# The inverse of the delta rule in 32-column diagonal blocks and corners, in place of 128-column products at every level

## The chip, the cores and the metric

The kernel is one program for one core of one Trainium2 chip. All data are fp32, except a few mask constants in bf16. The metric is the device time of one execution on that core in microseconds; a smaller number is better. Three executions of the kernel before took 4603.44, 4605.32 and 4605.34 us; their median is 4605.32 us.

TensorE (PE) multiplies a stationary block, which a weight load (PEld) brings in, with a moving block, and writes to PSUM. In this trace every fp32 product is two weight loads and two matmuls; a transpose with the identity is one of each. VectorE (DVE), ScalarE (ACT) and GpSimd (POOL) do elementwise work. Engines wait for each other by semaphores only.

## The reference, cut to what matters

The program runs a chain of stages: a modulation stage (Ada), a gated-delta-rule mixer (DeltaNet), Peer, attention, Peer, and then a second model part. The change touches the delta rule alone. Per head and per chunk of tokens the reference does

```python
gc = jnp.cumsum(gc, axis=-1)
decay = jnp.exp(jnp.where(incl, gc[..., :, None] - gc[..., None, :], -jnp.inf))
kk = jnp.einsum('bhid,bhjd->bhij', kc, kc)
a = eye + jnp.where(strict, kk * decay * bc[..., :, None], 0.0)
rhs = jnp.concatenate([vc * bc[..., None], kc * (bc * jnp.exp(gc))[..., None]], axis=-1)
sol = lax.linalg.triangular_solve(a, rhs, left_side=True, lower=True, unit_diagonal=True)
u, w = sol[..., :dv], sol[..., dv:]
v_new = u - jnp.einsum('bhcd,bhde->bhce', w, S)
qk = jnp.where(incl, jnp.einsum('bhid,bhjd->bhij', qc, kc) * decay, 0.0)
o = q_exp_gc @ S + qk @ v_new            # written as einsums
S = S * jnp.exp(g_last)[..., None] + k_decayed.T @ v_new
```

16 value heads of 128 channels, 512 tokens (256 context, 256 latent), forward and backward. The kernel takes chunks of 128 tokens, so there are four chunks per direction.

## The kernel before, in words

**Halves, chains, steps.** DeltaNet works on two halves of 8 heads, one after the other. Before the chain of a half there are projections, convolutions and norms, after it the gate projection and the output projection. Inside a half there are four chains, `self.chains`: two groups of 4 heads by two directions. Each chain has two PSUM banks, `two(ch)`, and eight buffers of 128 x (4 x 128), `self.bufs[ch]`: gL, D, DT, T, P, X, M1, S. The chains go through four steps `i` (chunks), and a step needs the state S that the step before left. Eight steps run in all, and in every phase of a step each engine takes the four chains one after the other.

**A step on TensorE** (`pe_chain`): `pe_decay` makes the decay exponents DT (4 products of 128x128) and D (one product with 512 moving columns); then k k^T (`kk`, L1001, 2 products per chain) and k q^T (`qk`, L1005); from the second step on k S (`kS`, L1014, 256 columns). Then comes the inverse of the unit triangular 128x128 matrix of each head, by doubling: for level l = 1 to 6, block size 2^l, X = (level's part of D)^T P (L1026) and Y = T^T X (L1037), each 4 products of 128x128 per chain, then P = P - Y on VectorE (L1222) and T = P transposed (L1175 on VectorE, by 32x32 blocks; before level 6 on TensorE, L212). Then v_new = P^T vb (`vn`, L1053), q S (`qS`, L1063), the output (`o`, L1068) and the new state (`S`, L1076).

**The other engines in a step.** ScalarE takes exp of D and DT (L1083) and copies X (L1099), T5 (L1104) and v_new (L1108) out of PSUM. GpSimd multiplies the masks with beta (L1124), then for each level masks D with that level's constant (L1133, 128 x 512, seven per chain), and scales the keys (L1139). VectorE multiplies D and DT by masks and by kk and qk (L1196 to L1207), makes T0 (L1211), kS times exp(gc) (L1217), and, in the levels, vb from v and kS (L1234, L1237); then the outputs, next decays and the state.

**What sets the order.** The order on each engine is the order of the Python loops. A phase starts on a chain when the semaphores it waits for have come. Where an instruction waits for more than one semaphore, all but one of the waits stand in an instruction of their own on the sequencer (EVENT_SEMAPHORE, one or two waits in each), and the last is on the next weight load. For instance L1022 is a wait for P ahead of X, L1024 the wait ahead of X of level 6, L1033 and L1035 are waits ahead of Y.

A line that is already there and matters for what follows, in the last stage S5 (`pe`, L2679): products with 32 output columns placed at a tile position, and in `drive` (L2652) products with 32 rows. In Ada, L525 are products with two moving columns. In DeltaNet, L788 are products with 16 moving columns.

Of the kernel before, what the change touches and what calls it, by code (L numbers as in the profile page):

```python
# [16 lines left out]
LEVELS = [1, 2, 4, 8, 16, 32, 64]  # L17
# [3 lines left out]
def constants():  # L21
# [6 lines left out]
        "sel32": (i[:, None] % 32 == np.arange(32)[None, :]) & (np.arange(32)[None, :] < 2),  # L28
        "par": np.stack([(i // 16) % 2 == 0, (i // 16) % 2 == 1, i < 64, i >= 64], 1),
# [8 lines left out]
    lev = []  # L38
    for s in LEVELS:
        m = (r // (2 * s) == c // (2 * s)) & ((r // s) % 2 == 1) & ((c // s) % 2 == 0)  # L40
        lev += [m, m.T]
    parts["lev"] = np.concatenate(lev, 1)
# [422 lines left out]
class Modulation:  # L465
# [15 lines left out]
    def key(self, n, k0):  # L481
        return ("ada", self.l, n, k0)
# [134 lines left out]
class DeltaNet(Stage):  # L617
    def __init__(self, k):
# [6 lines left out]
        self.lev = k.al(14 * 64).bitcast(BF16).rearrange("p (l m) -> p l m", l=14)  # L625
        self.cw = k.al2(32, 5)
        self.al_, self.be, self.g = (k.al3(4, 2, 16) for _ in range(3))
        self.egc, self.erl, self.egl = (k.al3(4, 2, 16) for _ in range(3))
# [6 lines left out]
        self.tmp = k.al(14 * 128)  # L635
# [9 lines left out]
        self.chains = list(self.bufs)  # L645
        k.top = work
# [26 lines left out]
    def pool(self, e):  # L673
# [3 lines left out]
        e.dma_start(self.tmp, i["consts"][:, o:o + 14 * 128]).then_inc(*self.l_lev.up("l"))  # L677
# [195 lines left out]
    def dve(self, e):  # L873
# [4 lines left out]
        e.tensor_copy(self.lev, self.tmp.rearrange("p (l m) -> p l m", l=14)).then_inc(*V.up())  # L878
# [16 lines left out]
        for half in range(2):  # L895
# [4 lines left out]
            for j, (kind, c, n) in enumerate(self.jobs(half)):  # L900
                if half == 0 and j == 8:
                    e.wait_ge(*self.S.at("sums"))
                    e.wait_ge(*self.S.at("be"))
                self.dve_keys(e, half, j)
# [55 lines left out]

    def masks(self, d):
        return [self.k.const(n) for n in (("le", "gt") if d == 0 else ("ge", "lt"))]
# [5 lines left out]
    def pe_decay(self, e, half, i, ch, names=("DT", "D")):  # L968
# [3 lines left out]
        for name in names:  # L972
            if i:
                e.wait_ge(*self.V.at((half, i - 1, ch, "O" if name == "DT" else "S")))
            if name == "DT":
                for h in range(4):
                    m = e.matmul(b1[:, h * 128:(h + 1) * 128], gL[:, h, :], le, start=True, stop=True)  # L977
            else:
                m = e.matmul(b0, le, gL.rearrange("p h n -> p (h n)"), start=True, stop=True)
            m.then_inc(*self.P.up((half, i, ch, name)))  # L980

    def pe_chain(self, e, half):
        P, V, S, G = self.P, self.V, self.S, self.G
        for i in range(4):
# [7 lines left out]
            for ch in self.chains:  # L992
                b0, b1 = self.two(ch)
                tok = self.place(half, ch, i)[1]
# [4 lines left out]
                for q in range(2):  # L999
                    kq = self.kT[:, ch[0] * 2 + q, tok]  # L1000
                    m = e.matmul(b0[:, q * 128:(q + 1) * 128], kq, kq, start=True, stop=True)  # L1001
                m.then_inc(*P.up(key("kk", ch)))
                e.wait_ge(*S.at(key("DT", ch)))
# [4 lines left out]
            for ch in self.chains:  # L1008
                b0, b1 = self.two(ch)
                if not first:  # L1010
# [6 lines left out]
            for l in range(1, 7):  # L1017
                for ch in self.chains:
                    gL, Pm = self.bufs[ch][0], self.bufs[ch][4]
                    b0, b1 = self.two(ch)  # L1020
                    e.wait_ge(*G.at(key(f"lev{l}", ch)))
                    e.wait_ge(*V.at(key(f"P{l - 1}", ch)))  # L1022
                    if l == 6:
                        e.wait_ge(*S.at(key("T5", ch)))  # L1024
                    for h in range(4):
                        m = e.matmul(b0[:, h * 128:(h + 1) * 128], gL[:, h, :], Pm[:, h, :], start=True, stop=True)  # L1026
                    m.then_inc(*P.up(key(f"X{l}", ch)))
                for ch in self.chains:
                    T, Xp = self.bufs[ch][3], self.bufs[ch][5]
                    b0, b1 = self.two(ch)  # L1030
                    e.wait_ge(*S.at(key(f"X{l}", ch)))
                    if l < 6:
                        e.wait_ge(*V.at(key(f"T{l - 1}", ch)))  # L1033
                    if l == 1:
                        e.wait_ge(*V.at(key("DTq" if first else "kSe", ch)))  # L1035
                    for h in range(4):
                        m = e.matmul(b1[:, h * 128:(h + 1) * 128], T[:, h, :], Xp[:, h, :], start=True, stop=True)  # L1037
                    m.then_inc(*P.up(key(f"Y{l}", ch)))
                if l == 5:
                    for ch in self.chains:  # L1040
                        Pm = self.bufs[ch][4]
                        b0, b1 = self.two(ch)
                        e.wait_ge(*V.at(key("P5", ch)))
                        for h in range(4):
                            m = self.turn(e, b0[:, h * 128:(h + 1) * 128], Pm[:, h, :])
                        m.then_inc(*P.up(key("T5", ch)))
            for ch in self.chains:
                Pm, M1 = self.bufs[ch][4], self.bufs[ch][6]
                b1 = self.two(ch)[1]
                e.wait_ge(*V.at(key("vb", ch)))  # L1050
                e.wait_ge(*V.at(key("P6", ch)))
# [3 lines left out]
            for ch in self.chains:  # L1055
# [3 lines left out]
                if not first:  # L1059
                    Sv = St.rearrange("p h n -> p (h n)")  # L1060
                    e.wait_ge(*S.at(key("X6", ch)))
# [16 lines left out]

    def act_decay(self, e, half, i, ch, names=("DT", "D")):
# [6 lines left out]
    def act_chain(self, e, half):  # L1086
        P, V, S, G = self.P, self.V, self.S, self.G
        for i in range(4):
# [6 lines left out]
            for l in range(1, 7):  # L1095
                for ch in self.chains:
                    b0 = self.two(ch)[0].rearrange("p (h n) -> p h n", h=4)
                    e.wait_ge(*P.at(key(f"X{l}", ch)))
                    e.activation(self.bufs[ch][5], b0, ACT.Copy, bias=0.0, scale=1.0).then_inc(*S.up(key(f"X{l}", ch)))  # L1099
                if l == 5:  # L1100
                    for ch in self.chains:
                        b0 = self.two(ch)[0].rearrange("p (h n) -> p h n", h=4)
                        e.wait_ge(*P.at(key("T5", ch)))
                        e.activation(self.bufs[ch][3], b0, ACT.Copy, bias=0.0, scale=1.0).then_inc(*S.up(key("T5", ch)))  # L1104
# [5 lines left out]
    def pool_chain(self, e, half):  # L1110
# [3 lines left out]
        for i in range(4):  # L1114
            first = i == 0
            key = lambda name, ch: (half, i, ch, name)
            for ch in self.chains:
                n, tok, h0 = self.place(half, ch, i)
                gt = self.masks(ch[1])[1]
                e.wait_ge(*P.at(key("DT", ch)))  # L1120
                if not first:
                    e.wait_ge(*V.at((half, i - 1, ch, "S")))
                    e.wait_ge(*G.at((half, i - 1, ch, "kr")))
                e.tensor_tensor(self.bufs[ch][6], rep(gt), self.be[:, n, ch[1], h0:h0 + 4].unsqueeze(2).to_broadcast([128, 4, 128]),  # L1124
                                MUL).then_inc(*G.up(key("bm", ch)))
            for l in range(7):
                for ch in self.chains:
                    gL, D = self.bufs[ch][3 if l == 0 else 0], self.bufs[ch][1]
                    if l == 0:
                        e.wait_ge(*V.at(key("Dk", ch)))  # L1130
                    elif l > 1:
                        e.wait_ge(*P.at(key(f"X{l - 1}", ch)))
# [1742 lines left out]
```

## Time and profile before

| | us |
|---|---|
| median of three executions | 4605.32 |
| the profiled execution | 4609.08 |
| its span, first to last instruction | 4607.3 |
| TensorE busy | 3848.6 (84%) |
| VectorE busy | 2793.2 (61%) |
| chain of half 0 (from 356 us to 663 us) | 307 |
| chain of half 1 (from 926 us to 1236 us) | 310 |

The granted clock is given as a share of 2.4 GHz: 1.00 is 2.4, 0.50 is 1.2. Busy times of TensorE count the pipeline's latency of each matmul, so the rate at which products come is read from the length of a row that merges many of them, divided by their number. "x32" on a row of the chain of waits counts weight loads and matmuls, so it is 16 matmuls, or 8 products.

### The profile page before, as it was taken

To read this page: it belongs to the slowest core of one execution; us is meant where nothing else is said; L and a number is where in the kernel's file an instruction comes from. 1 tells how busy PE (TensorE), PEld (TensorE's weight loads), DVE (VectorE), ACT (ScalarE), POOL (GpSimd) and SP (SyncE) were. 2 spreads that over 40 slices of the span, in tenths; PEclk is the share of its full clock that TensorE was granted. 3 is DMA by queue.
4 is the path that set the end of the run, shared out by engine and by line. 5 is a ranking of instruction groups with operands and counts; after the bars stand their busy time and mean duration, and the time that the engine had idled before them with its cause. 6 is when DMAs were issued, how large, how long until landed. Compare 5 with 4: busy or idle time off the path is not lost.

```text
span 4607.3 us, 42013 instructions
## 1 busy us (share of the span) xinstructions
PE 3848.6 (84%) x14279; PEld 2181.3 (47%) x14279; DVE 2793.2 (61%) x5932; ACT 987.5 (21%) x2441; POOL 1388.5 (30%) x1231
## 2 busy tenths in 40 slices
PE   6799999999998998777777769887777789875999
PEld 2448874488744443222222225543222358532684
DVE  1248882588836677777677744667776348448241
ACT  0133320322213222222222222222222121010100
POOL 1006530064303344444444420244444100027000
PEclk6699999999999999999999989999999889976999
DMA  9420002200039999999999961899999424320343
GB/s 370 139 64 1 1 10 82 65 1 1 13 102 357 403 416 421 419 418 414 410 416 415 411 269 64 315 416 419 419 412 416 143 83 140 124 77 1 131 148 126
DMA packets 269507, 1043.13 MB, mean 226 GB/s; under 512 B 19394, under 2 KB 103596, under 8 KB 170992
## 3 DMA queue, kind: packets, MB, share of 16 engines
q0 software_dynamic: 114832, 816.26, 43.4%
q1 hardware_dynamic: 154464, 224.18, 14.4%
q8 instruction: 117, 1.92, 0.2%
q14 instruction: 94, 0.77, 0.0%
HBM read 1039.29 MB, written 1.08 MB: 226 GB/s over the span
## 4 chain that ended last, share of the span: by engine, by line
PE 49%; DMA 25%; DVE 15%; POOL 5%; issue 3%; ACT 3%; DVEq 0%; POOLq 0%; ACTq 0%
DMA arena<-in_peer_uv,arena 23%; PE psum L261 13%; PE psum L1529 10%; PE psum L299 4%; PE psum L717 4%; PE psum L1487 3%; PE psum L756 2%; DVE arena L1664 2%; PE psum L212 2%; PE psum L1037 2%; DMA arena<-in_ada_w 2%; PE psum L1026 2%; POOL arena L1133 2%; DVE arena L1175 1%; DVE arena L1222 1%
## 5 line engine op out<-in xcount | busy, mean ns | idle before, releaser
L1529 PE MATMUL psum<-arena 128*128 128x512 f32 x3072 | 1447.0, 615 | 401.6 <-ACT arena L1564 398.1
L1664 DVE SCALAR_TENSOR_TENSOR arena<-arena 128x1024 bf16<-128x1024 f32 x768 | 941.5, 1226 | 518.8 <-DMA arena<-in_peer_uv,arena 479.4
L1622 POOL DMA_INDIRECT arena<-in_peer_uv,arena x768 | 866.0, 1128 | 1170.9 <-PE psum L1529 1029.8
L1529 PEld LDWEIGHTS psum<-arena 128*128 128x128 f32 x3072 | 568.8, 194 | 1230.1 <-ACT arena L1564 648.3
L261 PE MATMUL psum<-ring,arena 128*128 128x512 f32 (+2 forms) x1408 | 600.9, 591 | 30.1 <-DVE arena L2543 9.1
L261 PEld LDWEIGHTS psum<-ring,arena 128*128 128x128 f32 x1408 | 272.5, 202 | 352.7 <-issue 326.2
L1557 ACT ACTIVATE arena<-arena 128x2 f32<-128x2 f32 x384 | 78.2, 204 | 1241.8 <-DVE arena L1664 1241.7
L299 PE MATMUL psum<-arena,ring 128*128 128x256 f32 x1408 | 314.7, 385 | 9.1 <-DVE arena L2538 7.7
L1133 POOL TENSOR_TENSOR arena<-arena 128x512 f32<-128x512 f32 x224 | 284.0, 1293 | 110.0 <-PE psum L1026 71.1
L1564 ACT ACTIVATE arena<-consts,arena 128x128 f32<-128x128 f32 x768 | 268.3, 394 | 224.2 <-DVE arena L1676 221.1
L299 PEld LDWEIGHTS psum<-arena,ring 128*128 128x128 f32 x1408 | 270.5, 193 | 51.3 <-issue 8.0
L212 PE MATMUL psum<-consts,arena 128*128 128x128 f32 (+2 forms) x833 | 134.0, 309 | 141.7 <-DVE arena L362 75.7
L717 PE MATMUL psum<-arena,ring 128*128 128x512 f32 x512 | 228.6, 601 | 1.6 <-issue 1.6
L1026 PE MATMUL psum<-arena 128*128 128x128 f32 x1536 | 198.9, 283 | 31.7 <-POOL arena L1133 27.8
L1026 PEld LDWEIGHTS psum<-arena 128*128 128x128 f32 x1536 | 184.8, 196 | 43.7 <-POOL arena L1133 37.1
L212 PEld LDWEIGHTS psum<-consts,arena 128*128 128x128 f32 (+2 forms) x833 | 109.6, 160 | 200.8 <-issue 103.7
L1487 PE MATMUL psum<-arena,ring 128*128 128x128 f32 (+3 forms) x704 | 183.5, 412 | 9.1 <-ACT arena L1303 7.4
L1124 POOL TENSOR_TENSOR arena<-consts,arena 128x512 f32<-128x512 f32 x32 | 39.3, 1250 | 500.3 <-PE psum L977 472.7
L1037 PE MATMUL psum<-arena 128*128 128x128 f32 x1536 | 179.4, 275 | 0.0
L1099 ACT ACTIVATE arena<-psum 128x512 f32<-128x512 f32 x192 | 114.7, 597 | 286.4 <-PE psum L1026 285.3
L1037 PEld LDWEIGHTS psum<-arena 128*128 128x128 f32 x1536 | 175.4, 192 | 0.0
L1222 DVE TENSOR_TENSOR arena<-arena,psum 128x512 f32<-128x512 f32 x192 | 126.4, 666 | 60.4 <-PE psum L1037 60.1
(380 smaller groups left out, 3942.7 us busy)
## 6 DMA issues: line engine op xcount, KB each, us to landing
arena<-in_ada_w SPq DMA_DIRECT2D x48, 1024.0 KB, 14.4
ring<-in_ffn_w_up SPq DMA_DIRECT2D x44, 1024.0 KB, 5.1
ring<-in_dn_w_in SPq DMA_DIRECT2D x24, 1024.0 KB, 5.4
ring<-in_peer_w_query SPq DMA_DIRECT2D x22, 1024.0 KB, 6.7
ring<-in_ffn_w_down SPq DMA_DIRECT2D x20, 1024.0 KB, 5.0
arena<-in_peer_uv,arena POOLq DMA_INDIRECT x768, 12.8
ring<-in_ev_w_in SPq DMA_DIRECT2D x10, 1024.0 KB, 5.3
ring<-in_dn_w_out SPq DMA_DIRECT2D x8, 1024.0 KB, 4.8
```

The costliest lines, as they stand in the source:

```text
L212: return e.transpose(out, in_, self.k.const("ident")[0:n, 0:n])
L261: m = e.matmul(o, self.hT[:, k0 + k, t * 128:(t + 1) * 128], w[:, k, :], start=k0 + k == 0, stop=k0 + k == self.KC - 1)
L299: m = e.matmul(self.bank(c)[:, 0:self.nt], w[:, k, j * 128:(j + 1) * 128], self.hT[:, k, 0:self.nt], start=k == 0, stop=k == self.KC - 1)
L717: m = e.matmul(k.banks[j % 4], w[:, q, j % 2 * 128:(j % 2 + 1) * 128], self.hT[:, q, :], start=q == 0, stop=q == 7)
L1026: m = e.matmul(b0[:, h * 128:(h + 1) * 128], gL[:, h, :], Pm[:, h, :], start=True, stop=True)
L1037: m = e.matmul(b1[:, h * 128:(h + 1) * 128], T[:, h, :], Xp[:, h, :], start=True, stop=True)
L1133: e.tensor_tensor(gL, D, rep(self.lev[:, 2 * l + ch[1], :]), MUL).then_inc(*G.up(key(f"lev{l}", ch)))
L1487: m = e.matmul(k.banks[j % 2][:, 0:w_], w[:, n, c % 2 * 128:(c % 2 + 1) * 128], self.hT[:, n, a * 128:b * 128], start=n == 0, stop=n == 7)
L1529: m = e.matmul(k.banks[4 + t % 2 * 2 + nh], self.diag[g % self.ND], self.vsl[g % self.NS][:, nh * 512:(nh + 1) * 512], start=u % 8 == 0 an ...
L1564: e.activation(self.diag[g % self.ND], k.const("ident"), ACT.Copy, bias=0.0, scale=self.cf[u % 2][:, s:s + 1]).then_inc(*S.up(("dg", g)))
L1622: e.indirect_dma_start(self.uv[g % self.NS], None, self.table(), bass.IndirectOffsetOnAxis(ap=self.eid[u % 6][:, s:s + 1], axis=0)).then_i ...
L1664: e.scalar_tensor_tensor(self.junk[g % 2], self.us[g % self.NS], 1.0, self.h[:, u // 8, :], MUL, MUL, accum_out=self.a[u % 2][:, s:s + 1]) ...
```

## The change

The levels are kept in 32-column blocks. LEVELS shrinks to 1, 2, 4, 8, 16, so that level 0 and levels 1 to 4 work inside the four 32x32 diagonal blocks of each 128x128 matrix. T, P, D and X of these levels are 128 x (4 x 32) each, `self.small[ch]`. Each of the four blocks of each head has its own 32x32x32 product at tile position (32r, 32r). So X and Y of a level are 16 small products per chain in place of 4 full ones.

```diff
+            for l in range(1, 5):
+                for ch in self.chains:
+                    Tc, Pc, Dc, Xc = self.small[ch]
+                    X = self.two(ch)[0][:, 256:384].rearrange("p (h n) -> p h n", h=4)
+                    e.wait_ge(*G.at(key(f"lev{l}", ch)))
+                    e.wait_ge(*V.at(key(f"P{l - 1}", ch)))
+                    for h in range(4):
+                        for r in self.quarters():
+                            m = e.matmul(X[r, h, :], self.blocks[ch][r, l - 1, h, :], Pc[r, h, :], start=True, stop=True,
+                                         tile_position=(r.start, r.start))
+                    m.then_inc(*P.up(key(f"X{l}", ch)))
...
+                    for h in range(4):
+                        for r in self.quarters():
+                            m = e.matmul(Y[r, h, :], Tc[r, h, :], Xc[r, h, :], start=True, stop=True, tile_position=(r.start, r.start))
+                    m.then_inc(*P.up(key(f"Y{l}", ch)))
```

Rows and columns of D are stored by nearness (`near`): columns 0 to 31 hold the block on the diagonal, 32 to 63 its neighbour in the pair, 64 to 127 the other half. The D exponents and kk are made in this order, in ten pieces:

```diff
-                m = e.matmul(b0, le, gL.rearrange("p h n -> p (h n)"), start=True, stop=True)
+                for rows, cols, at in self.near():
+                    m = e.matmul(bv[rows, :, at], le[:, rows], gL[:, :, cols], start=True, stop=True, tile_position=(0, rows.start))
...
-                for q in range(2):
-                    kq = self.kT[:, ch[0] * 2 + q, tok]
-                    m = e.matmul(b0[:, q * 128:(q + 1) * 128], kq, kq, start=True, stop=True)
+                for rows, cols, at in self.near():
+                    for q in range(2):
+                        kq = self.kT[:, ch[0] * 2 + q, n * 128:(n + 1) * 128]
+                        m = e.matmul(bv[rows, q, at], kq[:, rows], kq[:, cols], start=True, stop=True, tile_position=(0, rows.start))
```

Eight of the ten pieces have 32 output rows, two have 64. Levels 5 and 6 touch only corners (`pe_corners`, new): X5 and Y5 are 8 products of 32x32x32 per chain each; T5, X6 and Y6 are 4 products of 64x64x64 per chain each, with the two directions of a head group taken in turn inside the loop over heads. They go straight into P: ScalarE writes the negated corner.

```diff
+        for pair in pairs:
+            for ch in pair:
+                e.wait_ge(*V.at(key("P4", ch)))
+                e.wait_ge(*V.at(key("Dk", ch)))
+            for h in range(4):
+                for ch in pair:
+                    D, Pc, X = self.bufs[ch][1], self.small[ch][1], wide(self.two(ch)[0][:, 256:384])
+                    for src, dst in self.corners(5, ch[1]):
+                        m = e.matmul(X[dst, h, :], D[src, h, 32:64], Pc[src, h, :], start=True, stop=True,
+                                     tile_position=(src.start, dst.start))
```

ScalarE also copies kk out of PSUM (128x256) and has two small copies each per chain for X5, P5 and for T and X of level 6, and one for P6; the copies of X1 to X4 are 128 x 128. GpSimd no longer makes the mask with beta; it makes bv = v times beta (128x512), the masked D of levels 1 to 4 from the 128x128 small D in two operations per chain (128 and 384 elements per partition), multiplies the rest of D with beta and DT with its mask, and copies the four diagonal blocks into P after level 4 (four copies per chain). On VectorE the small D, T0 and P0 are five operations on 128 x 128; P and T of levels 1 to 4 are 128x128 operations; one chain's Dk (384 elements) and DTq (512) stand after each level; P5, P6 and the vb operations inside the levels are gone:

```diff
+            for l in range(1, 5):
+                for ch in self.chains:
+                    Tc, Pc, Dc, Xc = self.small[ch]
+                    e.wait_ge(*P.at(key(f"Y{l}", ch)))
+                    e.tensor_tensor(Pc, Pc, v4(self.two(ch)[0][:, 384:512]), SUB).then_inc(*V.up(key(f"P{l}", ch)))
+                    e.wait_ge(*V.now())
+                    self.dve_turn(e, Pc, Tc).then_inc(*V.up(key(f"T{l}", ch)))
...
+                    e.tensor_tensor(M1, v4(self.two(ch)[1]), col(self.beg, ch), MUL).then_inc(*V.up())
+                    e.wait_ge(*G.at(key("bv", ch)))
+                    e.wait_ge(*V.now())
+                    e.tensor_tensor(M1, self.bv[ch], M1, SUB).then_inc(*V.up(key("vb", ch)))
```

kS moves on TensorE from before the levels to between level 4 and the corners, and its two operations on VectorE (the last lines above) with it. The first step uses bv as it is. `beg` is beta times exp(gc), made once. The level masks shrink to 320 columns in the constants.

## Rows read from the trace of the kernel before

**Rows 1.** Windows, half 0: us, busy per engine (instructions), PEclk, DMA.

```profile
...
344.00:420.00 76.00, 69.40 (x572) 67.69 (x573) 56.29 (x80) 25.52 (x44) 43.48 (x36) 0.93 0.00 1
...
582.00:663.00 81.00, 76.34 (x600) 70.40 (x599) 69.46 (x97) 23.57 (x40) 44.55 (x36) 1.00 0.00 1
...
```

**Rows 2.** Timeline, TensorE, fourth step's beginning: start us, length us, what, idle before.

```profile
...
581.87 3.74 PE L977 MATMUL psum<-consts,arena 128*128 128x128 f32 x32
585.44 3.60 PE L979 MATMUL psum<-arena,consts 128*128 128x512 f32 x8
588.88 0.61 PE L1001 MATMUL psum<-arena 128*128 128x128 f32 x4
...
592.00 0.61 PE L1005 MATMUL psum<-arena 128*128 128x128 f32 x4
593.95 4.72 PE L1014 MATMUL psum<-arena 128*128 128x256 f32 x16 [1.34 <-DVE arena L1207]
599.74 0.49 PE L1026 MATMUL psum<-arena 128*128 128x128 f32 x2 [1.07 <-POOL arena L1133]
```

**Rows 3.** Timeline, TensorE, same step from level 5 on.

```profile
...
632.04 3.14 PE L1026 MATMUL psum<-arena 128*128 128x128 f32 x24
...
639.91 1.91 PE L212 MATMUL psum<-consts,arena 128*128 128x128 f32 x16
...
645.23 3.74 PE L1037 MATMUL psum<-arena 128*128 128x128 f32 x32
648.80 3.74 PE L1053 MATMUL psum<-arena 128*128 128x128 f32 x32
...
659.40 3.88 PE L1076 MATMUL psum<-arena 128*128 128x128 f32 x32
```

**Rows 4.** Chain of waits, same step: start us, length us, what.

```profile
...
606.52 0.70 DVE arena L1222
...
614.55 0.61 DVE arena L1222
...
622.80 0.61 DVE arena L1222
...
630.67 0.61 DVE arena L1222
...
```

**Rows 5.** Timeline, TensorE, beginning of the first step.

```profile
...
349.62 0.61 PE L1001 MATMUL psum<-arena 128*128 128x128 f32 x4
...
359.96 5.25 PE L1026 MATMUL psum<-arena 128*128 128x128 f32 x23 [6.60 <-POOL arena L1133]
```

**Rows 6.** Timeline, VectorE, right after the chain of half 0.

```profile
...
667.44 0.68 DVE L920 TENSOR_SCALAR arena<-arena 128x128 f32<-128x128 f32 x3
```

**Rows 7.** Groups to 1300 us: count, busy us, mean ns, idle.

```profile
...
L1133 POOL TENSOR_TENSOR arena<-arena 128x512 f32<-128x512 f32 x224 | 284.0, 1293 | 110.0 <-PE psum L1026 71.1 <-DVE arena L1204 37.9
...
L1099 ACT ACTIVATE arena<-psum 128x512 f32<-128x512 f32 x192 | 114.7, 597 | 286.4 <-PE psum L1026 285.3
...
L866 ACT ACTIVATE arena<-psum 128x128 f32<-128x128 f32 x64 | 17.8, 278 | 17.9 <-PE psum L212 16.4
...
```

**Rows 8.** Timeline, TensorE, S5 with 32-column tiles.

```profile
...
4117.14 3.63 PE L2679 MATMUL psum<-arena 128*32 128x256 f32 x16 [6.38 <-POOL arena L2714]
...
```

**Rows 9.** Line L1035 alone: count, ns min/median/max, first and last start us.

```profile
...
L1035 PEldq EVENT_SEMAPHORE  x4: 51/51/51, 604.7 to 606.5; - x4
...
```

**Rows 10.** Line L1024 alone, the same columns.

```profile
...
L1024 PEldq EVENT_SEMAPHORE  x4: 51/51/51, 641.2 to 642.6; - x4
...
```

**Rows 11.** Line L1033 alone, the same columns.

```profile
...
L1033 PEldq EVENT_SEMAPHORE  x2: 51/51/51, 635.4 to 635.5; - x2
...
```

**Rows 12.** Windows with narrow products, columns of rows 1; the first is L525.

```profile
...
89.50:103.00 13.50, 13.50 (x65) 13.50 (x64) 0.50 (x1) 0.00 (x0) 0.00 (x0) 0.50 1.05 386
...
272.50:279.00 6.50, 6.50 (x49) 6.50 (x48) 0.00 (x0) 3.24 (x10) 0.00 (x0) 0.79 0.01 3
4117.00:4187.00 70.00, 41.80 (x192) 18.34 (x192) 62.93 (x82) 0.00 (x0) 59.14 (x49) 0.60 0.00 1
...
```

More of the change, by code:

```diff
@@ L1016, in pe_chain @@
                     m.then_inc(*P.up(key("kS", ch)))
[L1017 to L1046, printed above, removed]
+            self.pe_corners(e, half, i)
             for ch in self.chains:
-                Pm, M1 = self.bufs[ch][4], self.bufs[ch][6]
+                Pm, M1 = self.bufs[ch][4], self.bv[ch] if first else self.bufs[ch][6]
                 b1 = self.two(ch)[1]
-                e.wait_ge(*V.at(key("vb", ch)))
-                e.wait_ge(*V.at(key("P6", ch)))
+                if first:
+                    e.wait_ge(*G.at(key("bv", ch)))
+                    e.wait_ge(*V.at(key("DTq", ch)))
+                else:
+                    e.wait_ge(*V.at(key("vb", ch)))
+                e.wait_ge(*S.at(key("P6", ch)))
                 for h in range(4):
@@ L1098, in act_chain @@
                     e.wait_ge(*P.at(key(f"X{l}", ch)))
[L1099 to L1104, printed above, removed]
+                    e.activation(self.small[ch][3], wide(self.two(ch)[0][:, 256:384]), ACT.Copy, bias=0.0,
+                                 scale=1.0).then_inc(*S.up(key(f"X{l}", ch)))
@@ L1116, in pool_chain @@
             key = lambda name, ch: (half, i, ch, name)
+            beta = lambda ch, w: self.be[:, self.place(half, ch, i)[0], ch[1], half * 8 + ch[0] * 4:half * 8 + ch[0] * 4 + 4].unsqueeze(
+                2).to_broadcast([128, 4, w])
             for ch in self.chains:
[L1118 to L1132, printed above, removed]
-                    e.tensor_tensor(gL, D, rep(self.lev[:, 2 * l + ch[1], :]), MUL).then_inc(*G.up(key(f"lev{l}", ch)))
+                n = self.place(half, ch, i)[0]
@@ new lines, in pool_chain @@
+                if first:
+                    e.wait_ge(*P.at(key("DT", ch)))
+                    e.wait_ge(*S.at(("rows", half, 15)))
+                    e.memset(self.bufs[ch][4], 0.0).then_inc(*G.up(key("zero", ch)))
+                elif i == 1:
+                    e.wait_ge(*P.at((half, 0, ch, "vn")))
+                else:
+                    e.wait_ge(*V.at((half, i - 1, ch, "vb")))
+                e.tensor_tensor(self.bv[ch], self.vt[:, n, ch[0] * 4:ch[0] * 4 + 4, :], beta(ch, 128), MUL).then_inc(*G.up(key("bv", ch)))
@@ new lines, in pool_chain @@
+            for ch in self.chains:
+                D, DT = self.bufs[ch][1], self.bufs[ch][2]
+                e.tensor_tensor(D[:, :, 32:128], D[:, :, 32:128], beta(ch, 96), MUL).then_inc(*G.up(key("Db", ch)))
+                e.wait_ge(*S.at(key("DT", ch)))
+                e.tensor_tensor(DT, DT, rep(self.masks(ch[1])[0]), MUL).then_inc(*G.up(key("DTm", ch)))
+            for ch in self.chains:
+                Pm, Pc = self.bufs[ch][4], self.small[ch][1]
+                e.wait_ge(*V.at(key("P4", ch)))
+                if first:
+                    e.wait_ge(*G.at(key("zero", ch)))
+                else:
+                    e.wait_ge(*P.at((half, i - 1, ch, "vn")))
+                for r in self.quarters():
+                    e.wait_ge(*G.now())
+                    e.tensor_copy(Pm[r, :, r], Pc[r]).then_inc(*G.up(key("px", ch)))
@@ L1208, in dve_chain @@
-            for ch in self.chains:
-                T = self.bufs[ch][3]
-                e.wait_ge(*G.at(key("lev0", ch)))
-                e.tensor_tensor(T, rep(ident), T, SUB).then_inc(*V.up(key("T0", ch)))
-                e.wait_ge(*V.now())
-                self.dve_turn(e, ch, 3, 4).then_inc(*V.up(key("P0", ch)))
+                Tc, Pc, Dc, Xc = self.small[ch]
+                D, kk = self.bufs[ch][1], self.keys(ch)
+                n, tok, h0 = self.place(half, ch, i)
+                e.wait_ge(*S.at(key("kk", ch)))
```

223 lines of the change are left out of this document (166 added, 57 removed).

## The prediction

> **What bounds the kernel now.** I read the windows of the four steps first, then TensorE's timeline in one step, then the chain of waits there, and last the sequencer's own rows. A step after the first lasts 81 us, of which TensorE is busy 76.3 and VectorE 69.5, at a granted clock of 1.00 [rows 1]. There are eight steps, two of them first steps. In the fourth step, the front (DT, D, kk, qk, kS) takes from 581.87 to 599.74, 17.9 us, with 1.3 us of waiting ahead of kS and 1.1 us for the level masks of GpSimd [rows 2]. Levels 1 to 4 take from there to about 631.9, 32.2 us; X5 to Y6 with the transpose between them to 648.80, 16.9 us; v_new to the state 14.4 us [rows 3]. The reader is to see in the chain of waits that the levels 1 to 4 go by VectorE: its first P of one level and of the next stand 8.03, 8.25 and 7.87 us apart [rows 4], while 32 products on TensorE need 2 x 3.57 = 7.14 us. One full product costs 3.57/16 = 0.223 us: 16 of them fill the 3.57 us between the starts of Y6 and v_new [rows 3]. So the limit now is shared: VectorE in levels 1 to 4, TensorE from level 5 to the end. In the first step the levels start at 359.96, after 6.6 us in which TensorE waited for GpSimd's masks; kk had begun at 349.62 [rows 5].
>
> **What the change does to each.** VectorE's share goes. P and T of a level were two operations of 512 elements per chain; now they have 128, and three VectorE operations of 128 elements took 0.68 us, 0.23 each [rows 6]. That is 4 x 2 x 0.23 = 1.8 us a level, with one Dk and one DTq of at most 0.7 each: 3.3 us in place of 8. ScalarE's copies shrink from 597 to 278 ns, GpSimd's seven mask operations of 1293 ns become two on 128 and 384 elements, 1.3 us together in proportion [rows 7]. All of it fits beside TensorE if TensorE needs more than 3.3 us a level. So the question is what TensorE needs.
>
> **The price of a small product.** A 32x32x32 product has one quarter of the moving and one quarter of the stationary columns of a full one, and tiles beside each other overlap: in S5 16 matmuls of 256 columns in alternating column tiles took 3.63 us, 0.227 each [rows 8], at a clock of mostly 1.2 GHz. One full-width matmul of 128 columns takes 0.112 at 2.4 GHz (3.57/32), so 256 at 1.2 GHz would take 0.45: two tiles did run side by side. By streaming alone a level would thus be cheap. But each product is still two weight loads and two matmuls, and a level has 4 x 2 x 16 = 128 of them, 512 instructions, where before it had 32 products and 128 instructions. What does the sequencer need per instruction? Its own waits show it, where it runs ahead of the array. L1035 stands ahead of each chain's 16 instructions of Y1; the four are 1.8 us apart from first to last, 0.60 us a chain [rows 9], though the array takes 0.89 for the same 16. L1024, the same ahead of X6: 1.4 to 1.5 us over three intervals, about 0.49 each [rows 10]. A wait that is already met costs the sequencer some time too: two of L1033 with nothing between them stand 0.1 us apart, 51 ns of it the instruction [rows 11]. I take 0.13, which the rounding allows. That leaves (0.49 - 0.13)/16 = 23 ns and (0.60 - 0.13)/16 = 29 ns per instruction. I take 26 ns. The end below is 23; as the end above I take L1035's interval whole, 0.60/16 = 37 ns. The full products of today hide this, since an instruction of theirs takes 56 ns in the array. The small ones can't.
>
> The Trainium skill (TensorE: Matmul & The Clock Gate, on the 56 ns gap in Part 1) says that the starts of two matmuls never come closer than about 25 ns however small they are, and that the sequencer spends about 62 ns per matmul where it decodes in software. By the first a level's 256 matmuls would take an estimated 6.4 us, by the second 15.9. The trace, with 46 to 58 ns per pair of load and matmul, stands nearer to the second.
>
> **The sum, per step, on TensorE.** X or Y of a level, one chain: 64 x 0.026 + 0.13 = 1.79 us, where 0.89 were. Levels 1 to 4: 32 of these = 57.3 us against 32.2: +25.1. D: 10 products and 40 instructions per chain, 1.17 us, 4.7 with its waits, against 3.4: +1.3. kk: 20 products, 80 instructions, 2.2 us, 8.8 for four chains, against 1.8: +7.0. In a later step this fills the 2.4 us of waits of today's front, and kS (3.4 us) goes behind the levels: front 3.6 + 4.7 + 8.8 + 1.8 = 18.9 against 17.9, +1.0, and kS +3.4. Corners: X5 and Y5 are 32 instructions per chain, 8 x (0.83 + 0.06) = 7.1 us; T5, X6, Y6 are 16 per chain, 12 x (0.42 + 0.06) = 5.8; and three places where the first pair has nothing to do until ScalarE has copied, about 1 us each (two copies of 0.3 per chain and a hop [rows 7]): 16 against 16.9, -0.9. The tail of 14.4 stays. Sum for a later step: 25.1 + 1.0 + 3.4 - 0.9 = +28.6 us. In a first step kk fills the time in which TensorE waited for masks (kk and qk from 349.6 end at 360.2, and the levels began at 359.96), there is no kS, and 31.2 us of levels and 16.0 of corners stood before: 26 + 1.3 + 0 = +27.
>
> Edits at nothing: beg, the shorter masks, the memset, bv, the copies into P (16 small ones of GpSimd, bounded above by 0.4 us each = 6.4 us, a quarter of L1133's 1293 ns and some on top, beside X5 and Y5 of 7.1 us), the two VectorE operations behind kS (7 us of VectorE for four chains, beside kS 3.4 and corners 16; v_new waits for the last). Their cover is TensorE's long phases; without it, GpSimd's copies would put up to 6 us before T5.
>
> **The clock.** 13.5 us of products with two moving columns, back to back, left the granted clock at 0.50; 16 moving columns gave 0.79 over 6.5 us, and S5's 32-column tiles, busy 41.8 of 70 us, 0.60 [rows 12]. So I expect it to fall to 1.2 GHz in the 57 us of small products. The sequencer's price doesn't change with it (a guess: no row shows it apart); what follows, kS, the corners and v_new, does at twice the price until it has risen again. I take 3 us a step; the bounds are 0 and the whole of kS, the tail, DT and qk, 3.4 + 14.4 + 3.6 + 1.8 = 23 us.
>
> So (27 + 3) + 3 x (28.6 + 3) = 125 us a half, +249 for two. The profiled execution takes 4609.1 (span 4607.3); that gives 4858, and 4 us less against the median of 4605.3: **4855 us**. By 23 ns per instruction the levels take 50, kk 7.7, D 4.1, the corners 15: +19 in a later step, +17 in a first one, and with 2 us for the clock +164: 4770.
>
> **Rivals.**
>
> A. *An instruction costs 37 ns or more.* For it: L1035's whole interval. Against: L1024 has 31 with its wait. Levels 76.4 us, front +5.4, corners +2.9: +56 and +50 in a first step, with the clock 3 each: +460, 5065.
>
> B. *The clock stays at 1.2 GHz through the whole chain*, as in S5. For it: rows 12. Against: the tail, DT, D and qk are 20 us of dense full products, and the clock was 1.00 in such stretches. +23 in place of 3 in each step: 5015.
>
> C. *On the other side: small products come side by side without a price per instruction.* Then a level is bound by VectorE and the hops, about 4 us (3.3 and what a chain waits), four levels 16 in place of 32.2; the front loses its 2.4 us of waits, the corners are 2 shorter, kS adds 3.4: -17 a step, about 4470. It decides at the price where 512 instructions and 8 waits fill today's 8.05 us: (8.05 - 8 x 0.13)/512 = 14 ns. Against: two phases in which the sequencer needed 23 and 29. For: those had full operands behind them, and a queue that holds back the sequencer would look alike; S5's tiles did overlap. The Trainium skill (TensorEngine Tiling (Array Packing), Theoretical Speedup) promises up to 16 times where both dimensions are 32 or less; it is this case, and no row shows 32x32 tiles.
>
> D. *Nothing comes of it*: about 14 ns, the gain on VectorE and the loss on TensorE even out, within 0.2% (which is also about what a measurement can tell from no change), 4605.
>
> **Chances.** Forecast with 23 to 29 ns: 0.58. A: 0.12. B: 0.11. C: 0.13, with any price below 14 ns. D: 0.03; some price between 15 and 22, slower by less than 160: 0.03. So slower 0.84, same 0.03, faster 0.13. The range leaves out C and the worst of A and B: 4690 to 5070; the likeliest case's own is 4770 to 4940.
>
> **What would show it.** Right: X or Y of levels 1 to 4 at 1.6 to 2.1 us a chain on TensorE's timeline with no idle time in front of them; a step after the first of 100 to 120 us; VectorE's busy time in the window of a step down from 69 to about 50; the granted clock at 0.50 in the levels and back during the tail; kk at 2 us or more a chain. Wrong: small matmuls starting less than 28 ns apart in long rows, TensorE idle ahead of X of each level with VectorE or ScalarE as the releaser (C), or the tail at twice its length through to DT (B). If a step's corners take over 20 us, my hops there were too short.

## The result, and the profile after

The changed kernel takes 4558.74 us (median of 4, 4555.74 to 4564.14), the kernel before 4605.33 (4603.44 to 4606.32): ratio 0.990, 95% interval 0.9887 to 0.9912. The prediction was 4855, from 4690 to 5070, with 0.13 for faster: wrong in its sign.

Both chains of the delta rule became shorter, and nothing else did: the next projection (L261) starts at 645.00 instead of 667.41 behind half 0, and 549.40 instead of 573.08 us later behind half 1. These are 46.1 us; the medians differ by 46.6, the spans of the two profiled executions by 45.0. The windows of the four steps of half 0, to be held against [rows 1] (us, busy per engine with instructions in brackets, granted clock, DMA share, GB/s):

```profile
...
344.00:416.00 72.00, 51.17 (x1648) 46.35 (x1648) 29.96 (x72) 25.84 (x68) 33.06 (x48) 0.72 0.01 3
416.00:489.00 73.00, 54.48 (x1630) 48.32 (x1623) 39.04 (x89) 20.01 (x58) 27.98 (x40) 0.77 0.01 3
489.00:566.00 77.00, 57.49 (x1672) 50.67 (x1671) 39.76 (x92) 22.14 (x61) 26.98 (x40) 0.76 0.01 3
566.00:641.00 75.00, 54.31 (x1633) 47.33 (x1632) 36.29 (x84) 19.75 (x57) 23.67 (x36) 0.73 0.01 3
...
```

TensorE is no longer the engine that is always busy: 54 of 75 us, and VectorE 36 to 40. What it waits for says where the limit is. Its waits in these four steps (us in total, times, longest):

```profile
...
PE psum L1061 <- issue: 23.9, 13, 2.3
PE psum L1051 <- issue: 23.5, 13, 2.3
PE psum L1051 <- DVE arena L1318: 12.0, 9, 1.5
PE psum L1135 <- ACT arena L1210: 6.8, 8, 1.1
PE psum L1147 <- ACT arena L1215: 4.1, 7, 0.7
PE psum L1169 <- ACT arena L1222: 4.0, 8, 0.8
...
```

47.4 us lie ahead of X (L1051) and Y (L1061) of levels 1 to 4 with no engine to blame: no semaphore that the profile shows was late. (L1318 stands in VectorE's helper that turns P into T or T into P; ahead of X1 it makes P0.) TensorE's timeline of the fourth step, the one of [rows 2, 3], shows their pattern:

```profile
...
562.35 3.74 PE L1007 MATMUL psum<-consts,arena 128*128 128x128 f32 x32
566.02 4.70 PE L1011 MATMUL psum<-arena,consts 128*32 128x128 f32 x80
570.64 3.12 PE L1034 MATMUL psum<-arena 128*32 128x32 f32 x153
...
574.46 2.05 PE L1040 MATMUL psum<-arena 128*128 128x128 f32 x16
576.44 0.75 PE L1051 MATMUL psum<-arena 32*32 32x32 f32 x64
...
595.72 0.65 PE L1051 MATMUL psum<-arena 32*32 32x32 f32 x32 [2.33 <-issue]
596.13 1.51 PE L1061 MATMUL psum<-arena 32*32 32x32 f32 x94
599.27 0.77 PE L1061 MATMUL psum<-arena 32*32 32x32 f32 x34 [1.63 <-issue]
599.82 1.50 PE L1051 MATMUL psum<-arena 32*32 32x32 f32 x92
603.51 0.77 PE L1051 MATMUL psum<-arena 32*32 32x32 f32 x36 [2.20 <-issue]
...
608.53 6.26 PE L1069 MATMUL psum<-arena 128*128 128x256 f32 x16
614.72 0.81 PE L1123 MATMUL psum<-arena 32*32 32x32 f32 x64
...
625.37 4.77 PE L1083 MATMUL psum<-arena 128*128 128x128 f32 x32
...
637.00 3.88 PE L1106 MATMUL psum<-arena 128*128 128x128 f32 x32
```

```profile
...
GB/s 0 0 22 0 0 0 0 22 0 0 0 22 0 0 11 0 22 0 0 0 0 22 0 0 0 22 0 0 0 0 0 22 0 0 0 0 22 0 0 0
...
q8 instruction: 8, 0.13, 1.7%
q14 instruction: 1, 0.01, 0.1%
...
```

Eight packets of 16 KB in the 30 us, one every 3.4 to 4.1, are eight times 256 instructions of 64 bytes. In the whole execution this queue has 184 packets for 59212 instructions; the kernel before had 117 for 42013, so 67 packets came with 17199 instructions, 257 each. By the trace's own times the gaps go with the packets: packets that had landed at 981.08, 984.49, 987.97 and 991.30 us are followed by gaps that end at 982.27, 985.73, 989.19 and 992.65, 1.2 to 1.4 us later each time. The Trainium skill (Advanced Engine Details and Errata, ISA Cache) gives the line of the instruction cache as 16 KB, 256 instructions; the trace agrees.

So a level, 512 instructions, is two blocks, 7 to 8 us, and VectorE before needed 8.05 [rows 4]: in this step almost nothing was won or lost there. The gain stands around it. The fourth step by its starts on TensorE (what was predicted, what came, what stood before):

| part | predicted | after | before |
|---|---|---|---|
| DT, D, kk, qk | 3.6 + 4.7 + 8.8 + 1.8 = 18.9 | 3.7 + 4.6 + 3.8 + 2.0 = 14.1 | 17.9, kS in it |
| levels 1 to 4 | 57.3 | 32.1 | 32.3 |
| kS | 3.4 | 6.2 | |
| corners, levels 5 and 6 | 16 | 10.65 | 16.8 |
| v_new to S | 14.4 and 3 for the clock | 15.5 | 14.5 |
| step | 113 | 78.5 | 81.4 |

The levels took 27.9, 31.0 and 32.1 us in the later steps of half 0, and 30.0, 29.0 and 30.3 in those of half 1; the corners 10.5 to 10.9 everywhere but in first steps. In a first step the levels start 5.1 us earlier (354.88, [rows 5] had 359.96).

This fourth step has the smallest gain of the eight, 2.9 us; the others have 5.1 to 8.6. Over all eight, by the same starts, the corners went from 132.6 to 90.1 us, the levels from 256.3 to 243.5, the front with kS from 152.1 to 150.1, and v_new to S grew from 112.7 to 121.9. Most of what was gained is the corners.

### The profile page after: what moved, and what is told of

It is laid out like the page before. It is cut to its first block, busy times and chain, and to the rows that moved or that the text cites. A ratio compares the mean times of both kernels' runs of the same rounds, so it can differ in the third digit from the quotient of the medians.

```text
span 4562.3 us, 59212 instructions
## 1 busy us (share of the span) xinstructions
PE 3697.2 (81%) x22791; PEld 2016.6 (44%) x22791; DVE 2554.4 (56%) x5869; ACT 971.4 (21%) x2601; POOL 1243.6 (27%) x1271
## 3 DMA queue, kind: packets, MB, share of 16 engines
q1 hardware_dynamic: 154464, 224.18, 14.6%
## 4 chain that ended last, share of the span: by engine, by line
PE 50%; DMA 26%; DVE 11%; issue 5%; ACT 4%; POOL 3%; DVEq 0%; POOLq 0%; ACTq 0%; SPq 0%
DMA arena<-in_peer_uv,arena 24%; PE psum L261 13%; PE psum L1664 11%; PE psum L299 4%; PE psum L723 4%; PE psum L1622 3%; PE psum L762 2%; DVE arena L1799 2%; PE psum L212 2%; DMA arena<-in_ada_w 2%; PE psum L1061 1%; PE psum L1051 1%; POOL arena L2849 1%; PE psum L1083 1%; PE psum L1069 1%
## 5 line engine op out<-in xcount | busy, mean ns | idle before, releaser
L1664 PE MATMUL psum<-arena 128*128 128x512 f32 x3072 | 1462.6, 621 | 392.7 <-ACT arena L1699 389.0
L1757 POOL DMA_INDIRECT arena<-in_peer_uv,arena x768 | 853.7, 1112 | 1186.7 <-PE psum L1664 1045.7
L1664 PEld LDWEIGHTS psum<-arena 128*128 128x128 f32 x3072 | 575.8, 196 | 1230.4 <-ACT arena L1699 634.9
L261 PE MATMUL psum<-ring,arena 128*128 128x512 f32 (+2 forms) x1408 | 598.1, 589 | 30.1 <-DVE arena L2678 9.1
L261 PEld LDWEIGHTS psum<-ring,arena 128*128 128x128 f32 x1408 | 271.0, 201 | 351.3 <-issue 324.9
L299 PEld LDWEIGHTS psum<-arena,ring 128*128 128x128 f32 x1408 | 269.8, 193 | 50.9 <-issue 8.0
L212 PE MATMUL psum<-consts,arena 128*128 128x128 f32 (+3 forms) x705 | 117.9, 314 | 141.4 <-DVE arena L362 75.4
L212 PEld LDWEIGHTS psum<-consts,arena 128*128 128x128 f32 (+3 forms) x705 | 94.5, 162 | 198.9 <-issue 103.9
L1622 PEld LDWEIGHTS psum<-arena,ring 128*128 128x128 f32 x704 | 119.9, 199 | 77.5 <-issue 49.5
L723 PEld LDWEIGHTS psum<-arena,ring 128*128 128x128 f32 x512 | 97.5, 195 | 114.5 <-issue 114.5
L2842 POOL TENSOR_TENSOR arena<-arena 128x256 f32<-128x256 f32 x32 | 32.5, 1017 | 339.3 <-DVE arena L2866 339.3
L1051 PE MATMUL psum<-arena 32*32 32x32 f32 x4096 | 68.6, 228 | 69.6 <-issue 45.2
L329 ACT ACTIVATE arena<-x_res 128x1024 f32<-128x1024 f32 x10 | 10.6, 1058 | 507.0 <-DVE x_res L2685 319.3
L762 PE MATMUL psum<-ring,arena 128*128 128x512 f32 x256 | 110.4, 593 | 1.6 <-ACT arena L859 1.6
L1061 PE MATMUL psum<-arena 32*32 32x32 f32 x4096 | 69.3, 234 | 50.1 <-issue 50.1
## 6 DMA issues: line engine op xcount, KB each, us to landing
arena<-in_ada_w SPq DMA_DIRECT2D x48, 1024.0 KB, 14.4
arena<-in_peer_uv,arena POOLq DMA_INDIRECT x768, 12.9
```

Source lines behind the costliest of these rows:

```text
L212: return e.transpose(out, in_, self.k.const("ident")[0:n, 0:n])
L261: m = e.matmul(o, self.hT[:, k0 + k, t * 128:(t + 1) * 128], w[:, k, :], start=k0 + k == 0, stop=k0 + k == self.KC - 1)
L299: m = e.matmul(self.bank(c)[:, 0:self.nt], w[:, k, j * 128:(j + 1) * 128], self.hT[:, k, 0:self.nt], start=k == 0, stop=k == self.KC - 1)
L723: m = e.matmul(k.banks[j % 4], w[:, q, j % 2 * 128:(j % 2 + 1) * 128], self.hT[:, q, :], start=q == 0, stop=q == 7)
L762: m = e.matmul(k.banks[t * 2 + nh], self.oT[:, k0 + q, t * 128:(t + 1) * 128], w[:, q, nh * 512:(nh + 1) * 512], start=k0 + q == 0, stop=k ...
L1051: m = e.matmul(X[r, h, :], self.blocks[ch][r, l - 1, h, :], Pc[r, h, :], start=True, stop=True, tile_position=(r.start, r.start))
```

## The experiments

Two theories, for the levels. **F**: in the levels TensorE is bound by the arrival of code, block by block, whatever the products are. **H**: by the handing over between engines (P, T and X of a level wait for each other), and the gaps only look otherwise. **C** in the expectations below is not rival C of the prediction: it says that the array's own pace at the low clock sets the levels.

### Half of the products, and each one twice

```diff
-                        for r in self.quarters():
+                        for r in self.quarters()[:2]:        # e1_half
+                        for r in self.quarters() * 2:        # e2_twice
```

In X and Y of levels 1 to 4; waits, copies and VectorE's work stay.

> The changed kernel with only two of the four 32x32 blocks multiplied in X and Y of levels 1 to 4 (the other half of these products is left out, so the inverse is incomplete); all waits, copies and VectorE operations stay. The changed kernel's median is 4558.7 us; its levels 1 to 4 take 7.0 to 7.9 us each, in bursts of 256 TensorE instructions with 1.5 to 2.3 us of idle time behind each. Theory F (TensorE's instructions come in blocks of 256 that are fetched one after the other, 3.5 to 4 us a block whatever they do): a phase of four chains is 128 instructions, a level one block, 3.5 to 4 us, so about -3.6 x 32 = -115 us, 4445. Rival H (each level is a ring of waits TensorE-ScalarE-TensorE-VectorE and the idle time is that): only the bursts get shorter, 0.9 us a phase at most, and the idle time stays, 4558 - 0.9 x 64 = 4500 or less gain. Rival C (the clock at 1.2 GHz sets the pace of the array): as H.

Measured 4467.77, ratio 0.9698 (0.9678 to 0.9717): 91 us less than the changed kernel, of 8192 instructions and 32 packets of code (152 for 184). Theory F had asked for 114, H for 59 at most: 91 lies between, nearer to F. A level is now one block, and the waits for issue are all but gone from L1061 and down to a fifth at L1051, whose wait for VectorE's P0 ahead of X1 stays (24.4 us in the changed kernel, 25.1 here). In the second step of half 1 the four levels take 5.5, 4.4, 4.1 and 4.3 us where the changed kernel's take 8.0, 7.0, 7.0 and 8.1; F had 3.6 less for each. (TensorE matmuls: busy us, mean ns, idle before, released by; the changed kernel, then e1_half.)

```profile
...
L1051 PE MATMUL psum<-arena 32*32 32x32 f32 x4096 | 68.6, 228 | 69.6 <-issue 45.2
...
L1061 PE MATMUL psum<-arena 32*32 32x32 f32 x4096 | 69.3, 234 | 50.1 <-issue 50.1
...
```

```profile
...
L1051 PE MATMUL psum<-arena 32*32 32x32 f32 x2048 | 64.3, 227 | 35.0 <-DVE arena L1318 25.1 <-issue 9.3 <-POOL arena L1263 0.5
L1061 PE MATMUL psum<-arena 32*32 32x32 f32 x2048 | 61.1, 231 | 2.0 <-issue 1.9
...
```

> The changed kernel with each small product of X and Y of levels 1 to 4 made twice (same operands, same result). Theory F: 512 instructions a phase, a level four blocks, 14 to 15.5 us in place of 7 to 7.9: +7.3 x 32 = +235 us, about 4790. Rival H (ring of waits): only the bursts get longer by 1.9 us a phase and the pause stays once: +1.9 x 64 = +120, about 4680. Rival C (array's pace at 1.2 GHz): as H.

Measured 4791.35, ratio 1.040 (1.0379 to 1.0421): +232.6 us for 4 x 512 x 8 = 16384 instructions, 14.2 ns each, and 64 packets more (248), which is 16384/256. F had 235, H and C 120. The other engines do exactly what they did, so H falls; C falls with it, since TensorE's matmuls stand still for half of the time. TensorE's timeline in a level:

```profile
...
1036.26 1.92 PE L1051 MATMUL psum<-arena 32*32 32x32 f32 x127 [1.58 <-issue]
1040.03 1.01 PE L1051 MATMUL psum<-arena 32*32 32x32 f32 x58 [1.84 <-issue]
...
1043.80 1.93 PE L1061 MATMUL psum<-arena 32*32 32x32 f32 x127 [1.84 <-issue]
1047.57 1.01 PE L1061 MATMUL psum<-arena 32*32 32x32 f32 x59 [1.85 <-issue]
...
```

Every block of 128 pairs takes 3.77 us, half of it idle, though X depends on nothing new in the middle of its own phase.

### kS into the gaps

The kS products of chains 0, 1 and 2 behind X and Y of levels 2, 3 and 4, that of chain 3 where all four stood. Behind level 4 is directly ahead of that place, so only the chains 0 and 1 get in between levels:

```diff
+                if not first and l >= 2:
+                    self.pe_ks(e, half, i, self.chains[l - 2])
```

> The changed kernel with kS of the first three chains moved on TensorE into the levels, one behind Y of each of the levels 2 to 4; the last stays ahead of the corners. Theory F: kS is 16 instructions per chain (0.9 us of array at 2.4 GHz, 1.5 at 1.2) and the levels have 1.5 to 2.3 us of idle time per 256 instructions, so inside them it costs 16/256 of a block, 0.23 us, in place of 1.5: about -3.5 us in each of the six later steps, -21 us, about 4538. Rival H: the same products would sit in the ring and cost their 1.5 us each there: no change, 4558.

Measured 4555.34, ratio 0.989 (0.9873 to 0.9906), not to be told from the changed kernel. The median is H's 4558 and not F's 4538. But half of kS left its place, not three quarters, so F's own -21 would be some -14; and the four executions lie 9 us apart (4550.89 to 4560.03), those of the changed kernel 8. In the two profiled executions the stretches from X1 to X5 of the six later steps take 202.3 us here and 215.6 in the changed kernel, 13 less. Whether that is kS or the spread of the blocks' times from one execution to the next, one trace each can't tell: the run decides nothing between F and H. The timeline shows kS in a gap, and the next gap as long as before:

```profile
...
982.78 1.07 PE L1061 MATMUL psum<-arena 32*32 32x32 f32 x60 [2.09 <-issue]
983.78 2.07 PE L1109 MATMUL psum<-arena 128*128 128x256 f32 x4
985.78 2.05 PE L1051 MATMUL psum<-arena 32*32 32x32 f32 x128
987.60 0.98 PE L1061 MATMUL psum<-arena 32*32 32x32 f32 x60
990.60 0.87 PE L1061 MATMUL psum<-arena 32*32 32x32 f32 x68 [2.02 <-issue]
...
999.76 3.23 PE L1109 MATMUL psum<-arena 128*128 128x256 f32 x8
...
```

Two blocks took 7.82 us (982.78 to 990.60); the changed kernel's two at the same place took 6.92 (982.27 to 989.19). One gap is filled, but kS takes 2.0 us and not the 1.5 of a chain outside. The last line is kS of chain 2 with that of chain 3 behind it.

### A full product among the small ones, and the same on one tile

```diff
+                    e.matmul(self.two(ch)[0][:, 0:128], self.k.const("ident"), self.kT[:, 0, 0:128],
+                             start=True, stop=True)                               # e4_dummy
+                    e.matmul(self.two(ch)[0][0:32, 0:128], self.k.const("ident")[0:32, 0:32],
+                             self.kT[0:32, 0, 0:128], start=True, stop=True, tile_position=(0, 0))   # e6_small
```

One each ahead of the 16 products of every chain in X and Y of levels 1 to 4, 256 in all.

> The changed kernel with one 128x128x128 product of constants and keys (result unused, 4 instructions) ahead of the small products of each chain in X and Y of levels 1 to 4. It keeps the array busier. Theory F: +16 instructions in 256 of a phase, +0.22 us x 64 = +14 us; if the granted clock stays at 2.4 GHz through the levels then kS, the corners and v_new lose their 2.5 + 1 + 1 us a step, -30: about 4540; if the clock stays low, 4573. Rival C (the clock sets the pace of the levels): with the clock at 2.4 the levels get shorter by a third or more, -70 us or more, under 4490.

Measured 4647.61, ratio 1.0087 (1.007 to 1.0105): 89 us more, above every expectation. F had let the dummy cost 14 us at most. It did not keep the clock up either: the granted clock is 0.50 from 979 to 987 us, in level 4, so the run says nothing on C, for which it was made. The gaps are gone, the array itself now needs 1.3 us per chain and phase.

> The dummy of e4_dummy again, at the same 256 places (one ahead of the small products of each chain in every X and Y of the four levels, 8 steps), with the same 128 columns, but as a product on one 32x32 tile instead of the whole 128x128 array. e4_dummy cost 89 us over the changed kernel (4558.7), 0.35 us per dummy. Theory M (what e4 paid for is the change between whole-array products and tiles, twice per dummy; 128 columns by themselves are 0.05 to 0.11 us and one more instruction 15 ns): without the change of tiling only the columns and the instruction are left, and tiles of other rows can run beside them, so +5 to +35 us: 4565 to 4595. Theory W (what e4 paid for is the dummy itself, its columns at the low clock, its place in a bank that another engine reads, or the queue): the same 0.35 us: 4640 to 4655.

Measured 4573.30, ratio 0.9926 (0.9911 to 0.9941): +14.6 us, theory M. Of the 89 us, 74 come with the whole array in place of one tile, 0.29 us for each of the 256 dummies. First e4_dummy, then e6_small, one chain of Y:

```profile
...
982.40 0.65 PE L1063 MATMUL psum<-arena 32*32 32x32 f32 x32
982.98 0.80 PE L1060 MATMUL psum<-arena,consts 128*128 128x128 f32 x2
983.70 0.65 PE L1063 MATMUL psum<-arena 32*32 32x32 f32 x32
...
```

```profile
...
985.46 0.40 PE L1060 MATMUL psum<-arena,consts 32*32 32x128 f32 x1
985.46 0.33 PE L1063 MATMUL psum<-arena 32*32 32x32 f32 x6
985.65 0.42 PE L1060 MATMUL psum<-arena,consts 32*32 32x128 f32 x1
985.87 0.63 PE L1063 MATMUL psum<-arena 32*32 32x32 f32 x26
986.31 0.40 PE L1060 MATMUL psum<-arena,consts 32*32 32x128 f32 x1
...
```

A chain with its dummy lasts 1.30 us (982.40 to 983.70) in the one and 0.85 (985.46 to 986.31) in the other: 0.45 us for a change there and back, some 0.22 each, of which the gaps hid a part. In e6_small small products start within 0.01 us of the dummy, in e4_dummy 0.7 us behind it. The two dummies have the same 128 moving columns, but 128 and 32 stationary ones: what the longer weight loads cost by themselves was not taken apart from the change. The Trainium skill (TensorEngine Tiling (Array Packing), Key Properties) says that changing the tiling mode drains TensorE; the pair agrees. It would also account for the 2.0 us of kS in e3_ks, which has four more such changes a step; that was not taken apart and stays open.

### 64-column blocks for six levels

```diff
-LEVELS = [1, 2, 4, 8, 16]
+LEVELS = [1, 2, 4, 8, 16, 32]
...
-        return [slice(32 * b, 32 * b + 32) for b in range(4)]
+        return [slice(64 * b, 64 * b + 64) for b in range(2)]
...
-            for l in range(1, 5):
+            for l in range(1, 6):
```

> A version of its own that computes the reference: diagonal blocks of 64 columns for the first six levels (1 to 32), each level's X and Y as 64x64x64 products two at a time, so 8 instead of 16 products per chain and phase (128 instead of 256 TensorE instructions for the four chains); decay and kk in two pieces each for D's 64 near columns; the copies, the mask products and the P and T updates on 128x256 instead of 128x128; the block masks made one level ahead on POOL; one corner level (32 columns' X5 and Y5) fewer. Theory F (a level of the changed kernel is set by the arrival of 256-instruction blocks of code, 3.5 to 4.1 us per 256, 7.0 to 7.9 us for a level's 512): a level needs one block, 3.5 to 4.1 us, as in e1_half, and VectorE's two updates of 128x256 on four chains are then the bound, some 4.1 to 4.8 us (the updates of 128x512 took 0.87 to 1.0 each of 8 in the 8.05 us level of the kernel before, those of 128x128 some 0.28). Five levels 21 to 24 us instead of four levels and X5/Y5 in 30 to 31, front 2 us less: -7 to -11 us a step, 4470 to 4505. Theory H (what a level costs goes by the handing over between the engines, not by instructions: each of the 5 levels would keep its 7 us): 5 x 7.3 = 36.5 instead of 31, +4 us a step: 4580 to 4610.

Measured 4471.90 (4468.58 to 4478.63), ratio 0.971 (0.9697 to 0.9723): 133 us below the kernel before and 87 below the changed one. TensorE's timeline:

```profile
...
988.74 0.68 PE L1047 MATMUL psum<-arena 64*64 64x64 f32 x16 [0.56 <-DVE arena L1285]
991.25 0.88 PE L1047 MATMUL psum<-arena 64*64 64x64 f32 x16 [1.83 <-DVE arena L1285]
993.77 1.12 PE L1047 MATMUL psum<-arena 64*64 64x64 f32 x16 [1.63 <-DVE arena L1285]
996.28 1.12 PE L1047 MATMUL psum<-arena 64*64 64x64 f32 x16 [1.40 <-POOL arena L1231]
997.16 3.65 PE L1057 MATMUL psum<-arena 64*64 64x64 f32 x64
...
1004.88 2.42 PE L1047 MATMUL psum<-arena 64*64 64x64 f32 x64
1007.10 2.06 PE L1057 MATMUL psum<-arena 64*64 64x64 f32 x64
1008.97 2.44 PE L1047 MATMUL psum<-arena 64*64 64x64 f32 x64
...
1017.31 3.72 PE L1065 MATMUL psum<-arena 128*128 128x256 f32 x16
...
```

Levels 3 and 4 take 4.1 us each without a gap, as F had it and against H's 7.3. In 1000 to 1017 us VectorE is busy 15.4 of 17, and the granted clock is 0.95 where the changed kernel has 0.56 in its levels (576 to 608). The time came out in F's range, but not by its terms. The five levels take 28.7 us in the fourth step of half 0, not 21 to 24, because X1 goes chain by chain at the pace of VectorE and GpSimd, 2.5 us each; the changed kernel's levels with X5 and Y5 take 36.3, not 30 to 31. Beyond that, kS takes 3.65 us in place of 6.2, which I had not counted: the clock was still up behind the 64-column products. From D to v_new this step lasts 45.5 us and not 59.4: front -2.2, levels -3.4, kS -2.5, corners -5.7.

## Why the prediction was wrong

- **The step that failed is the price of a small product**, 26 ns for each of its instructions, from the intervals between the sequencer's waits [rows 9, 10]. In the changed kernel the same kind of wait (L1058, ahead of Y) has 64 small instructions between two, and the three in this row are 0.43 us apart each:

```profile
...
L1058 PEldq EVENT_SEMAPHORE  x3: 51/51/51, 986.3 to 987.2; - x3
...
```

  That is 7 ns per instruction, wait included. What I had read as the sequencer's own need was time in which it stood behind a queue of full products: the prediction named this reading against itself in rival C and gave it 0.13. That the queue held it back is argued, not shown by a run; that 26 ns was not a need is shown. What bounds a long run of small products in its place is the arrival of code, 3.5 to 4.3 us per 256 instructions: 1.0 us per chain and phase in this step, where the sum had 1.79.
- **The other half of that step** was to take a price per instruction as constant. The levels pay 14 to 16 ns on average (e2_twice: 14.2), as bursts and gaps. kk pays 10 without a gap, 320 instructions in 3.24 us in most steps. Of the error of 34.5 us in the fourth step, 25.2 are the levels, 5.0 kk, 5.3 the corners; kS and the tail are 0.9 the other way. The corners' waits for ScalarE were about right, 3.9 us for 3; their instructions took 6.8 and not 12.9. So the sum had the corners at -0.9 us a step where they gave -6.1, and they carry most of the gain.
- **The break-even** of 14 ns per instruction was right, and it is where the levels came to lie: 32.1 us for 32.3. With it the case was open, and the sign hung on the corners and the front.
- **D**, 4.7 us, measured 4.6, was right for another reason: 160 instructions at 29 ns. Its matmuls have 128 or 256 moving columns and take 58 ns each, where those of kk with 32 or 64 take 20; that the columns set it is argued.
- **The clock** fell to 1.2 GHz in the levels and rose in the tail, as said; 3 us a step were taken, and kS (6.2 for 3.65 behind the 64-column products) and v_new (4.6 for 3.6 before) cost 3.6. Rival B, the low clock through the whole step, did not come: it is back at 0.93 in 625 to 641.
- **Rivals**: C had the side and the mechanism for TensorE's array, and one of its signs came, small matmuls less than 28 ns apart; but TensorE's idle time had no releaser, and its limit, VectorE's 4 us a level, was not reached: the changed kernel is 89 us above its 4470, which e1_half with half of the products comes to, and e5_b64 with 64-column blocks. A fell. D, about 14 ns, was the nearest in the levels, and its 4605 missed what the corners gave.
- **Edits at nothing** held: no wait for them stands in the four steps. A wait that the sum had not stands elsewhere: for P0, made by VectorE (L1318), 12.0 us ahead of X1 in the four steps, where TensorE before had waited 14.0 us for GpSimd's masks (two of these waits in [rows 2, 5]). VectorE's busy time fell to 36 to 40 us in a later step, further than the 50 that were named.
- **Slips in the working**, without weight for the outcome: at 23 ns the levels come to 51.3 us by the sum's own terms, not 50, which makes the lower end about 4780; and levels 1 to 4 before ended at 632.04, not 631.9.

## What to carry over

Before many small products are put in place of few large ones, count TensorE's instructions: a long run of them goes at the pace at which blocks of 256 arrive, 3.5 to 4.3 us each here, however little the array has to do. Of the three block sizes that were run, 64 columns was the best: a level's 256 instructions came in the 4.1 us in which VectorE was 15.4 of 17 us busy, while 32 columns waited for code and 128 for VectorE. That such a balance is best elsewhere too is a guess. And an interval between two events of an engine that has a full queue in front of it is no price; look for a stretch where the queue is empty, or keep the chance of the reading that you can't exclude high.

## What the runs showed of the hardware

- A 32x32 matmul and its weight load pass in about 14 ns while code is there (64 matmuls from 996.12 to 996.99 in the second step of half 1). The Trainium skill (TensorE: Matmul & The Clock Gate, Part 1) has 25 ns as the least distance of two matmuls; with four tiles in turn the trace is below it, and the measurement decides; the 62 ns of the other decode path were nowhere near.
- 256 instructions of code per packet of 16 KB; 32 packets fewer for 8192 instructions fewer (e1_half), 64 more for 16384 more (e2_twice). One block each 3.46 to 4.32 us in a run of small products, 3.77 in e2_twice, with the gap's end 1.2 to 1.6 us behind the packet's landing.
- A change between whole-array products and 32x32 tiles takes some 0.22 us of TensorE's time at the low clock (e4_dummy against e6_small), with whatever the longer weight loads add in it.
- 32x32 products let the granted clock fall to 1.2 GHz (0.50 from 985 to 995 us, 0.56 in the levels' window of 576 to 608), 64x64 ones, two at a time, left it at 0.95 (e5_b64, 1000 to 1017).
